# Attention by one head and 128 queries a step, and gates ahead of the branches, in a trunk layer on one Trainium2 core

## The chip, the cores and the metric

The kernel runs on one core of a Trainium2 chip. The metric is the device time of one call in microseconds (us). Each version is run several times on the same chip; a profiled execution beside them gives the trace from which all rows below come. Its times are measured from the start of its span.

## The reference

One layer of a streaming encoder over 1024 positions and 1024 channels, all in float32. A token mixer with three branches is followed by a squared-ReLU MLP; each part is closed by a residual and a layer norm. What matters here is the mixer:

```python
u = layer_norm(x) * (1 + sc_m) + sh_m
z = u @ w_in[l]
z_pool, z_q, z_k, z_v, z_conv, z_gate = jnp.split(z, IN_SPLITS, axis=-1)
y_pool = pool_mixer(z_pool, ...) @ w_br_pool[l]
y_attn = chunk_attention(z_q, z_k, z_v, rel_bias[l]) @ w_br_attn[l]
y_conv = conv_module(z_conv, ...) @ w_br_conv[l]
gates = jax.nn.sigmoid(z_gate + b_gate[l]).reshape(B, S, N_BRANCH, D_MODEL)
merged = gates[:, :, 0] * y_pool + gates[:, :, 1] * y_attn + gates[:, :, 2] * y_conv
mix_out = merged @ w_o[l]
...
# chunk_attention: 8 heads of 64, chunks of 64 queries, keys of the own chunk and 8 before (576)
s = jnp.einsum('bnqhd,bnkhd->bnhqk', q, kb)          # + relative bias, NEG_INF before position 0
p = jax.nn.softmax(s, axis=-1)
o = jnp.einsum('bnhqk,bnkhd->bnqhd', p, vb)
# conv_module: GLU, a depthwise causal convolution of 31 taps on 256 channels, layer norm, swish
```

## The kernel before, in words

Every engine has its own program, written out by hand; semaphores order them against each other. No scheduler is at work: an engine executes its instructions in the order of the code, and waits where the code says `wait_ge`.

TensorE multiplies float32 values as two parts of reduced precision, `x_hi` and `x_lo`. The helper `product` (L1974 to L1976) issues three matmuls for each product: hi by hi, lo by hi, hi by lo. The parts are made in pairs: ScalarE (ACT) copies a raw tile into `_hi`, then VectorE (DVE) subtracts it from the raw tile into `_lo` ("cutting"; weights of `w_in` and of the branches come in blocks of 128 columns, `w_raw`, `w_hi`, `w_lo`, two slots each).

The stages up to the MLP are: the first norm and the projections for pooling and convolution; the projections q, k, v of the first head pair; **attention**; **gates and branches**; the product with `w_o`.

*Attention* is a loop over 64 steps `a` (4 head pairs by 16 chunks). A step takes 64 queries of two heads: their q columns stand block by block in a tile whose other halves are zero (`q_hi`, `q_lo`; GpSimd zeroes them in `zero_q`), so one matmul of 128 rows computes both heads. A step on PE is `scores` (one product, two for the full width of 576 keys in halves of 288), half of `between`, every second step `weigh` (for each block of 128 keys a product of 256 columns), `transpose_probs` of the step before, and the other half of `between`. `between` issues matmuls of 512 columns which project q, k, v for the next pair: 9 a step in the first three pairs, 6 in the last one, where two gate blocks are made ahead (`EARLY`). A gate block is the z_gate projection for 128 channels, 48 matmuls.

On DVE a step adds the bias to the scores and takes the row's maximum (`add_scores`' place, L1523); ACT makes the exponential and the row sum (L997); DVE takes the reciprocal (L1537) and scales the probabilities (L1538); PE transposes them; ACT copies the transposed tile into `pt_hi`, DVE subtracts it into `pt_lo` (L1544). Into nearly every step DVE puts one tap of the convolution (L1428, 62 in all). Six times in a pair DVE cuts half a projection (`take_half_lo`), three times a weight block (`cut_lo`, L1325).

*Gates and branches*: after attention, for each of 8 blocks of 128 channels, PE makes three gate blocks and the three branch products, ACT the sigmoids, DVE the products of both and their sum `mid` (L1602, L1609).

GpSimd (POOL) prepares sums for the MLP: 16 steps in which it loads 256 rows of `w_ff2` (`tw_rows`), multiplies them by the gate row (L778), forms three sums (L783 to L788) and stores them to DRAM (`tw_scratch`). They begin once the first gates, the convolution and the branch inputs are done (L769's waits), so they lie beside gates and branches.

## Time and profile before

| | us |
|---|---|
| device time, median of 3 (lowest, highest) | 1448.37 (1446.94, 1448.57) |
| span of the profiled execution | 1445.0 |
| PE busy | 1426.1 (99%) |
| DVE busy | 966.1 (67%) |
| ACT busy | 586.8 (41%) |
| POOL busy | 455.4 (32%) |

PE's clock was granted in full throughout (a row of 9s), and 96% of the chain that ended last is PE. A busy share of 99% does not say that PE runs at its peak: a matmul's record includes the time in which it overlaps its neighbour. What a matmul occupies is read from the distance between two starts.

In time: attention is 157 to 394 us, gates and branches 394 to about 660 us, POOL's 16 steps 453 to 671 us.

### The profile page before, as it was taken

Reading aid. Unit: us, or ns where it says so; the run is one execution under the profiler, and the core shown is the slowest. Engines: PE = TensorE matmul, PEld = TensorE weight load, DVE = VectorE, ACT = ScalarE, POOL = GpSimd, SP = SyncE. Lnnn points to the kernel's source line nnn. Section 1 sums busy time; section 2 is a strip of 40 time slices with the busy share of each in tenths; the row PEclk is TensorE's granted clock in tenths of the full one; section 3 lists DMA queues with packets and bytes.
Section 4 is the critical chain, followed back from the end, with each engine's and each line's share of the span. In section 5 each row is a group of like instructions: output and inputs, shape, how many; then the busy total and the mean of one; then the engine's idle time right before and its main releaser. Section 6 shows DMA issues by size and latency. Waiting matters only on the chain.

```text
span 1445.0 us, 17546 instructions
## 1 busy us (share of the span) xinstructions
PE 1426.1 (99%) x6770; PEld 1175.9 (81%) x6770; DVE 966.1 (67%) x1242; ACT 586.8 (41%) x829; POOL 455.4 (32%) x381
## 2 busy tenths in 40 slices
PE   7999999999999999999999999999999999999997
PEld 1788888888878888888888898888888888888886
DVE  4888888887785355453468888666555744575594
ACT  3412455555562112112435765444444544443251
POOL 1003500000004889895014415533443302040011
PEclk9999999999999999999999999999999999999999
DMA  9873111101014676776451283544445868576361
GB/s 349 295 265 114 31 30 38 38 16 32 16 44 162 245 259 249 255 268 218 131 204 59 88 277 131 175 154 160 156 137 192 277 243 306 210 233 231 113 224 58
DMA packets 149267, 241.49 MB, mean 167 GB/s; under 512 B 9480, under 2 KB 79550, under 8 KB 147144
## 3 DMA queue, kind: packets, MB, share of 16 engines
q1 hardware_dynamic: 134968, 177.04, 36.7%
q0 software_dynamic: 14224, 63.45, 11.6%
q8 instruction: 47, 0.77, 0.2%
q14 instruction: 28, 0.23, 0.1%
HBM read 170.17 MB, written 70.29 MB: 166 GB/s over the span
## 4 chain that ended last, share of the span: by engine, by line
PE 96%; DVE 1%; DMA 1%; SPq 1%; ACT 0%; issue 0%; DVEq 0%
PE ps L1974 27%; PE ps L1976 27%; PE ps L1975 27%; PE ps L2102 10%; PE ps L2158 2%; DMA mid<-in_x_dram 1%; PE ps L2041 1%; PE ps L2328 0%; SPq L455 0%; DVE bn L1331 0%; PE ps L1993 0%; PE ps L2123 0%; PE ps L2017 0%; PE ps L2200 0%; PE ps L2194 0%; PE ps L2022 0%
## 5 line engine op out<-in xcount | busy, mean ns | idle before, releaser
L1974 PE MATMUL ps<-act_hi,w_hi 128*128 128x512 f32 (+1 forms) x512 | 198.0, 387 | 0.0
L1976 PE MATMUL ps<-act_hi,w_lo 128*128 128x512 f32 (+1 forms) x512 | 196.0, 383 | 0.0
L1975 PE MATMUL ps<-act_lo,w_hi 128*128 128x512 f32 (+1 forms) x512 | 195.9, 383 | 0.0
L1839 DVE TENSOR_TENSOR part_lo<-k_raw,part_hi 128x1024 fp32r<-128x1024 f32 x112 | 153.9, 1414 | 48.2 <-ACT part_hi L872 46.5
L1974 PE MATMUL ps<-part_hi 128*128 128x512 f32 x448 | 174.3, 389 | 0.0
L1975 PE MATMUL ps<-part_lo,part_hi 128*128 128x512 f32 x448 | 174.3, 389 | 0.0
L1976 PE MATMUL ps<-part_hi,part_lo 128*128 128x512 f32 x448 | 174.3, 389 | 0.0
L872 ACT ACTIVATE part_hi<-k_raw 128x1024 fp32r<-128x1024 f32 x112 | 116.3, 1059 | 108.6 <-DMA k_raw<-tw_scratch 84.5
L1571 DVE TENSOR_TENSOR w_lo<-w_raw,w_hi 128x1024 fp32r<-128x1024 f32 x30 | 73.1, 2436 | 123.9 <-ACT w_hi L872 123.8
L1974 PEld LDWEIGHTS ps<-act_hi,w_hi 128*128 128x128 f32 x512 | 96.2, 188 | 19.7 <-issue 1.4
L1975 PEld LDWEIGHTS ps<-act_lo,w_hi 128*128 128x128 f32 x512 | 96.3, 188 | 19.1 <-issue 0.7
L1976 PEld LDWEIGHTS ps<-act_hi,w_lo 128*128 128x128 f32 x512 | 96.2, 188 | 18.9
L1975 PEld LDWEIGHTS ps<-part_lo,part_hi 128*128 128x128 f32 x448 | 84.1, 188 | 17.6
L1974 PEld LDWEIGHTS ps<-part_hi 128*128 128x128 f32 x448 | 84.1, 188 | 17.4
L1976 PEld LDWEIGHTS ps<-part_hi,part_lo 128*128 128x128 f32 x448 | 84.1, 188 | 17.4
L2102 PE MATMUL ps<-act_lo,w_hi 128*128 128x512 f32 x224 | 92.0, 411 | 0.0
L1251 ACT ACTIVATE h_buf<-h_buf,cols 128x1024 f32<-128x1024 f32 x28 | 32.3, 1152 | 144.7 <-DVE h_buf L1834 144.7
L2102 PE MATMUL ps<-act_hi,w_hi 128*128 128x512 f32 x224 | 90.7, 405 | 0.1
L2102 PE MATMUL ps<-act_hi,w_lo 128*128 128x512 f32 x224 | 87.9, 392 | 0.0
L872 ACT ACTIVATE w_hi<-w_raw 128x1024 fp32r<-128x1024 f32 (+1 forms) x53 | 55.6, 1049 | 78.4 <-PE ps L1976 77.3
L1974 PE MATMUL ps<-act_hi,set_hi 128*128 128x512 f32 x224 | 87.1, 389 | 0.0
L1975 PE MATMUL ps<-act_lo,set_hi 128*128 128x512 f32 x224 | 87.1, 389 | 0.0
(261 smaller groups left out, 3243.3 us busy)
## 6 DMA issues: line engine op xcount, KB each, us to landing
k_raw<-h_scratch SPq DMA_DIRECT2D x112, 256.0 KB, 4.0
k_raw<-tw_scratch SPq DMA_DIRECT2D x112, 256.0 KB, 5.0
ada<-in_w_ada_dram SPq DMA_DIRECT2D x11, 2048.0 KB, 8.8
w_raw<-in_w_in_dram SPq DMA_DIRECT2D x42, 512.0 KB, 4.2
tw_rows<-in_w_ff_dram POOLq DMA_DIRECT2D x16, 1024.0 KB, 5.5
tw_scratch<-tw_rows POOLq DMA_DIRECT2D x16, 1024.0 KB, 4.2
h_scratch<-h_sum POOLq DMA_DIRECT2D x64, 256.0 KB, 2.8
pair_raw<-in_w_ff_dram SPq DMA_DIRECT2D x13, 1024.0 KB, 6.0
```

What stands on the lines that cost most here:

```text
L872: return nc.scalar.activation(out, in_, ACT.Copy, **kw)
L1251: nc.scalar.activation(row, row, ACT.Relu, bias=cols[:, R_FF1 + n:R_FF1 + n + 1]).then_inc(relu_done, 1)
L1571: nc.vector.tensor_tensor(w_lo[b % 2][:, :, :], w_raw[b % 2][:, :, :], f(w_hi[b % 2][:, :, :]), ALU.subtract).then_inc(w_lo_done, 1)
L1839: nc.vector.tensor_tensor(part_lo[s][:, :, :], k_raw[rs][:, :, :], f(part_hi[s][:, :, :]), ALU.subtract)\
L1974: nc.tensor.matmul(out, sh, mh, start=first, stop=False)
L1975: nc.tensor.matmul(out, sh, ml, start=False, stop=False)
L1976: return nc.tensor.matmul(out, sl, mh, start=False, stop=last)
L2041: ins = nc.tensor.transpose(ps[:, 2 * (k % 2) + i // 4, (i % 4) * P:(i % 4 + 1) * P], mid[:, i, k * P:(k + 1) * P], ident[:, :])
L2102: ins = nc.tensor.matmul(ps[:, hz % 2, :], s, v, start=kk == 0, stop=kk == 23)
L2158: ins = nc.tensor.transpose(banks(6)[:, b * P:(b + 1) * P], probs[a % 2][:, cs], ident[:, :])
```

## The change

**Attention.** A step is now one head and 128 queries, 64 steps again (pair, head, tile of 128 queries). The scores span 640 keys for 128 queries; the corners outside a query's 576 keys are masked with -1e30 in the bias tile. A tile `qs` holds q's hi part in one head's 64 rows and its lo part in the other 64; `kd` holds the keys twice, in both halves of rows, so one matmul of 128 rows adds q_hi k and q_lo k. The second copy of the keys is made by DMAs within the on-chip memory (`double_keys`, four of 256 KB a pair). Scores are 2 matmuls a part instead of 3. `vs` holds V hi and V lo side by side as the 128 columns of one head, so that `weigh` is one matmul of 256 columns a block of keys; it now stands in every step. The output comes out in pieces: ACT copies one (`take_low`) and DVE adds two (`add_o`). Normalising stays on DVE.

**Projections and gates.** `between` issues 9 matmuls a step in all four pairs (`EARLY` is 3). Behind attention come 18 gate blocks of 48 matmuls (the first within the last two rounds of the attention loop), whose sigmoids are stored to DRAM (512 KB each) and read back; then 8 branch blocks; then the last three gates. The taps are taken out of attention and put between the cuts of the gate blocks.

**GpSimd.** `zero_q` is gone. The `w_ff2` sums are made in 32 steps of half the size, and start when the pooling means are done and the gate rows are stored.

```diff
-EARLY = 2
+EARLY = N_BRANCH
+PIECE = HALF // 2
+TAPS_IN = {0: 5, 1: 2, **{g: 7 for g in range(2, 9)}, 9: 6}
...
             def scores(a):
...
-                    ins = product(ps[:, 4 + part, 0:n],
-                                  ((q_hi[s][:, i, :], q_lo[s][:, i, :]), (k_hi[s][:, ks], k_lo[s][:, ks])),
-                                  True, True)
+                    for term in range(2):
+                        ins = nc.tensor.matmul(ps[:, 4 + part, 0:n], qs[s][:, h, t * P:(t + 1) * P], kd[s][:, term, h, ks],
+                                               start=term == 0, stop=term == 1)
...
-                    ins = product(ps[:, 2, 0:2 * P],
-                                  ((v_hi[s][:, kt, :], v_lo[s][:, kt, :]), (pt_hi[:, pb, :, :], pt_lo[:, pb, :, :])),
-                                  b == 0, b == nb - 1)
+                for m in range(nb):
+                    ins = nc.tensor.matmul(ps[:, 2, (b % 2) * 2 * P:(b % 2 + 1) * 2 * P], vs[s][:, t + 1 - nb + m, h * P:(h + 1) * P],
+                                           pt[:, b % 2, m, :, :], start=m == 0, stop=m == nb - 1)
...
+            def add_o(b):
+
+                pair, h, t = step_of(b)
+                rows = head_rows(h)
+                out = mid[rows, 2 + pair, t * P:(t + 1) * P]
+                dve.wait_ge(o_low_done, b + 1)
+                nc.vector.tensor_tensor(out, o_bank(b, rows, 0), out, ALU.add).then_inc(o_added, 1)
+                dve.wait_ge(o_added, 2 * b + 1)
+                nc.vector.tensor_tensor(out, o_bank(b, rows, 1), out, ALU.add).then_inc(o_added, 1)
...
+            for a in range(N_STEPS + 2):
+                pair, h, t = step_of(a)
                 if a < N_STEPS:
+                    add_scores(a)
+                if half_of(a - 1):
+                    take_half_lo(*half_of(a - 1))
...
+                    nc.vector.reciprocal(inv_sum[:, col:col + 1], row_sum[:, col:col + 1]).then_inc(inv_done, 1)
+                    dve.wait_ge(inv_done, a + 1)
+                    nc.vector.tensor_scalar(probs[a % 2][:, 0:w], probs[a % 2][:, 0:w], inv_sum[:, col:col + 1], None,
+                                            ALU.mult).then_inc(probs_done, 1)
+                if a >= 2:
+                    add_o(a - 2)
+                if 1 <= a <= N_STEPS:
+                    take_pt_lo(a - 1)
...
+            for g in range(G_BLOCKS):
+                cut_lo(N_G + 2 + g)
+                if g == 1:
+                    for k in BR_ORDER[:4]:
+                        cut_branch_lo(k)
+                for n in itertools.islice(taps, TAPS_IN.get(g, 0)):
+                    conv_tap(n)
...
@@ on GpSimd
-            pool.wait_ge(sig_done, EARLY)
-            pool.wait_ge(conv_done, 2)
-            pool.wait_ge(br_lo_done, KT)
-            pool.wait_ge(y_done, 3)
...
+            pool.wait_ge(scratch_stored, 48)
+            pool.wait_ge(means_summed, 8)
+            load_piece(0)
             load_rows(0)
-            for p in range(FF_PAIRS):
+            for u in range(TW_STEPS):
...
@@ on SyncE
+                if m < N_BRANCH:
+                    sp.wait_ge(conv_done, 2)
+                    sp.wait_ge(tw_stored, 32 * TW_STEPS)
```

PE, a full-width step of attention, before (`k_hi`, `q_hi` are the scores' operands, `act`, `w` those of the projections, L2158 the transposes; such steps carry a `weigh` every second time, 15 matmuls `ps<-pt_hi,v_hi`, `pt_lo,v_hi`, `pt_hi,v_lo` of 256 columns):

```order
L1974 MATMUL ps<-k_hi_75,q_hi_71 128x288 [waits biased]
L1975 MATMUL ps<-k_lo_77,q_hi_71 128x288
L1976 MATMUL ps<-k_hi_75,q_lo_73 128x288
L1974 MATMUL ps<-k_hi_75,q_hi_71 128x288
L1975 MATMUL ps<-k_lo_77,q_hi_71 128x288
L1976 MATMUL ps<-k_hi_75,q_lo_73 128x288
L2102 MATMUL ps<-act_hi,w_hi_54 128x512 [waits h_free1]
L2102 MATMUL ps<-act_lo,w_hi_54 128x512
L2102 MATMUL ps<-act_hi,w_lo_56 128x512
L2102 MATMUL ps<-act_hi,w_hi_54 128x512
L2158 MATMUL ps<-ident,probs_86 128x128 [waits pt_lo_done,probs_done]
L2158 MATMUL ps<-ident,probs_86 128x128 x3
```

and PE after, the same place (L2110 scores, L2070 projections, L2135 `weigh`, L2120 transposes):

```order
L2110 MATMUL ps<-kd_73,qs_71 128x320 [waits biased]
L2110 MATMUL ps<-kd_73,qs_71 128x320 x3
L2070 MATMUL ps<-act_hi,w_hi_55 128x512
L2070 MATMUL ps<-act_lo,w_hi_55 128x512
L2070 MATMUL ps<-act_hi,w_lo_57 128x512
L2070 MATMUL ps<-act_hi,w_hi_55 128x512
L2135 MATMUL ps<-pt,vs_75 128x256 [waits o_added,pt_lo_done]
L2135 MATMUL ps<-pt,vs_75 128x256 x2
L2120 MATMUL ps<-ident,probs_80 128x128 [waits pt_lo_done,probs_done]
L2120 MATMUL ps<-ident,probs_80 128x128 x3
L2070 MATMUL ps<-act_lo,w_hi_55 128x512
```

Six score matmuls of 288 columns have become four of 320, and `weigh` stands in each step with 3 to 5 matmuls of 256 columns.

DVE, one full-width step of attention before, beginning with the bias addition:

```order
L1523 ISA probs_85,neg_max<-ps,bias_rev_83 128x576 [waits pt_done,scores_done]
L1523 ISA neg_max 128x1
L1428 SCALAR_TENSOR_TENSOR mid<-h_pad,cols,mid 128x1024 [waits tap_done]
L1537 RECIPROCAL inv_sum<-row_sum 128x1 [waits exp_done]
L1538 TENSOR_SCALAR probs_85<-probs_85,inv_sum 128x576 [waits dve_step]
L1544 TENSOR_TENSOR pt_lo<-ps,pt_hi 128x5x128 [waits pt_hi_done]
```

and after:

```order
L1493 ISA probs_80,neg_max<-ps,bias_rev_78 128x640 [waits pt_done,scores_done]
L1493 ISA neg_max 128x1
L1529 RECIPROCAL inv_sum<-row_sum 128x1 [waits exp_done]
L1531 TENSOR_SCALAR probs_80<-probs_80,inv_sum 128x640 [waits inv_done]
L1503 TENSOR_TENSOR mid<-ps,mid 64x128 [waits o_low_done]
L1505 TENSOR_TENSOR mid<-ps,mid 64x128 [waits o_added]
L1511 TENSOR_TENSOR pt<-ps,pt 128x5x128 [waits pt_hi_done]
```

The tap has gone, the scaling is 64 columns wider, and the two additions from PSUM into `mid` stand ahead of the subtraction that PE's next `weigh` waits for.

DVE in the gate stage after, from the second gate block on (L1309 cuts a weight block, L1412 is a tap):

```order
L1309 TENSOR_TENSOR w_lo_57<-w_raw_53,w_hi_55 128x1024 [waits w_hi_done]
L1408 TENSOR_SCALAR conv_acc<-h_pad,cols 128x1024
L1412 SCALAR_TENSOR_TENSOR conv_acc<-h_pad,cols,conv_acc 128x1024 [waits tap_done] x4
L1309 TENSOR_TENSOR w_lo_56<-w_raw_52,w_hi_54 128x1024 [waits w_hi_done]
L1547 TENSOR_TENSOR br_lo<-mid,br_hi 128x1024 [waits br_hi_done] x4
L1412 SCALAR_TENSOR_TENSOR conv_acc<-h_pad,cols,conv_acc 128x1024 [waits tap_done] x2
L1309 TENSOR_TENSOR w_lo_57<-w_raw_53,w_hi_55 128x1024 [waits w_hi_done]
L1412 SCALAR_TENSOR_TENSOR conv_acc<-h_pad,cols,conv_acc 128x1024 [waits tap_done] x7
L1309 TENSOR_TENSOR w_lo_56<-w_raw_52,w_hi_54 128x1024 [waits w_hi_done]
L1412 SCALAR_TENSOR_TENSOR conv_acc<-h_pad,cols,conv_acc 128x1024 [waits tap_done] x7
```

The taps stand between the cuts of the weights, seven to a gate block from the third on.

POOL before, behind the zeroing of q (`gate_row` is the row of gate values, `tw_rows` the rows of `w_ff2`):

```order
L734 MEMSET q_hi_72 64x16x64 x2
L734 MEMSET q_lo_74 64x16x64 x2
L757 MEMSET w_pool_bd 128x256 [waits scores_done,q_zeroed]
L769 DMA gate_row<-gate_scratch 128x1024 [waits br_lo_done,conv_done,y_done,sig_done,consts_done]
L767 DMA tw_rows_143<-in_w_ff_dram 128x2x1024
L778 TENSOR_TENSOR tw_rows_143<-tw_rows_143,gate_row 128x1024 [waits tw_in]
L778 TENSOR_TENSOR tw_rows_143<-tw_rows_143,gate_row 128x1024
```

and after, behind the pooling means:

```order
L756 TENSOR_TENSOR mid<-mid 64x16 [waits means_summed]
L756 TENSOR_TENSOR mid<-mid 64x16
L777 DMA gate_piece<-gate_scratch 128x256 [waits means_summed,scratch_stored]
L777 DMA gate_piece<-gate_scratch 128x256
L786 DMA tw_rows_143<-in_w_ff_dram 128x2x256 x2
L799 TENSOR_TENSOR tw_rows_143<-tw_rows_143,gate_piece 128x512 [waits tw_in]
L799 TENSOR_TENSOR tw_rows_143<-tw_rows_143,gate_piece 128x512
L786 DMA tw_rows_144<-in_w_ff_dram 128x2x256 [waits tw_summed]
L786 DMA tw_rows_144<-in_w_ff_dram 128x2x256
L807 TENSOR_TENSOR tw_sum_145<-tw_rows_143 128x256
L809 TENSOR_TENSOR tw_sum_145<-tw_rows_143,tw_sum_145 128x256 [waits tw_summed]
```

The first load of `w_ff2` rows no longer waits for the branches; it stands right behind the means, and each operation covers half as many columns.

## Rows read from the trace of the kernel before

**Rows 1.** Busy time by stretch: us, PE, PEld, DVE, ACT, POOL busy, PEclk, DMA share, GB/s.

```profile
0.00:35.00 35.00, 24.60 (x64) 6.13 (x65) 14.04 (x44) 12.50 (x18) 4.11 (x40) 1.00 0.97 348
...
216.00:277.60 61.60, 61.60 (x376) 54.63 (x375) 52.35 (x106) 32.63 (x78) 0.00 (x0) 1.00 0.11 31
```

**Rows 2.** PE's timeline: start us, duration us, engine, line, operation.

```profile
203.83 0.28 PE L1974 MATMUL ps<-pt_hi,v_hi 128*128 128x256 f32 x1
203.95 0.28 PE L1975 MATMUL ps<-pt_lo,v_hi 128*128 128x256 f32 x1
...
207.10 0.40 PE L2102 MATMUL ps<-act_hi,w_lo 128*128 128x512 f32 x1
207.33 0.30 PE L1974 MATMUL ps<-k_hi,q_hi 128*128 128x288 f32 x1
207.46 0.29 PE L1975 MATMUL ps<-k_lo,q_hi 128*128 128x288 f32 x1
```

**Rows 3.** PE's groups by form, whole span: busy us, mean ns, idle before.

```profile
L1976 PE MATMUL ps<-pt_hi,v_lo 128*128 128x256 f32 x120 | 33.9, 282 | 0.0
L1976 PE MATMUL ps<-k_hi,q_lo 128*128 128x288 f32 x64 | 18.9, 295 | 0.0
```

**Rows 4.** PE's timeline, first gate matmul behind attention.

```profile
396.59 0.79 PE L1974 MATMUL ps<-act_hi,w_hi 128*128 128x512 f32 x1
```

**Rows 5.** DVE's timeline, attention steps of 192 and 576 columns, last pair.

```profile
342.59 0.68 DVE L1485 TENSOR_TENSOR v_lo<-ps,v_hi 128x512 fp32r<-128x512 f32 x1
343.19 1.22 DVE L1325 TENSOR_TENSOR w_lo<-w_raw,w_hi 128x1024 fp32r<-128x1024 f32 x1
...
347.02 0.35 DVE L1523 CUSTOM_DVE_ANT_0 probs<-ps,bias_rev 128x192 f32<-128x192 f32 x1
...
348.43 0.28 DVE L1544 TENSOR_TENSOR pt_lo<-ps,pt_hi 128x128 fp32r<-128x128 f32 x1
348.63 0.41 DVE L1523 CUSTOM_DVE_ANT_0 probs<-ps,bias_rev 128x256 f32<-128x256 f32 x1
...
366.35 0.75 DVE L1523 CUSTOM_DVE_ANT_0 probs<-ps,bias_rev 128x576 f32<-128x576 f32 x1
...
368.05 0.17 DVE L1537 RECIPROCAL inv_sum<-row_sum 128x1 f32<-128x1 f32 x1 [0.94 <-ACT probs L997]
368.25 0.52 DVE L1538 TENSOR_SCALAR probs<-probs,inv_sum 128x576 f32<-128x576 f32 x1
368.68 0.82 DVE L1544 TENSOR_TENSOR pt_lo<-ps,pt_hi 128x640 fp32r<-128x640 f32 x1
369.42 0.75 DVE L1523 CUSTOM_DVE_ANT_0 probs<-ps,bias_rev 128x576 f32<-128x576 f32 x1
```

**Rows 6.** Timelines of POOL and DVE where both are busy.

```profile
161.68 1.95 POOL L734 MEMSET q_lo<- 64x1024 f32 x2
162.70 1.02 DVE L1538 TENSOR_SCALAR probs<-probs,inv_sum 128x128 f32<-128x128 f32 x1
...
508.04 4.75 POOL L778 TENSOR_TENSOR tw_rows<-tw_rows,gate_row 128x1024 f32<-128x1024 f32 x2
508.03 5.85 DVE L1609 TENSOR_TENSOR mid<-mid,tmp 128x1024 f32 x1
514.27 1.30 POOL L783 TENSOR_TENSOR tw_sum<-tw_rows 128x512 f32<-128x512 f32 x1
```

**Rows 7.** DVE's groups by form, 455 to 662 us: busy us, mean ns, idle before.

```profile
L1571 DVE TENSOR_TENSOR w_lo<-w_raw,w_hi 128x1024 fp32r<-128x1024 f32 x19 | 59.0, 3105 | 95.2 <-ACT w_hi L872 95.2
L1602 DVE TENSOR_TENSOR tmp<-ps,gate 128x1024 f32<-128x1024 f32 x10 | 12.2, 1225 | 12.3 <-PE ps L1976 11.7
```

**Rows 8.** POOL's timeline, multiplications of its first and its sixteenth step.

```profile
453.58 4.75 POOL L778 TENSOR_TENSOR tw_rows<-tw_rows,gate_row 128x1024 f32<-128x1024 f32 x2 [7.36 <-DMA tw_rows<-in_w_ff_dram]
...
657.23 4.75 POOL L778 TENSOR_TENSOR tw_rows<-tw_rows,gate_row 128x1024 f32<-128x1024 f32 x2
```

**Rows 9.** DVE's timeline, four taps in a row.

```profile
395.23 5.24 DVE L1428 SCALAR_TENSOR_TENSOR mid<-h_pad,cols,mid 128x1024 f32<-128x1024 f32 x4
```

More of the change, by code:

```diff
@@ L491, in _ @@
             load_block(9)
[L492 removed]
+            heads_before = {14: 2, 16: 3, 17: 4, 19: 5, 20: 6, 21: 7}
+            for n in range(10, N_G + 4):
                 if n == 12:
@@ L1111, in cut_row_hi @@
+            for j in range(LAST):
+                cut_hi(N_BR + 2 + j)
             def cut_row_hi(k):
@@ L1529, in _ @@
+            for a in range(N_STEPS + 2):
+                pair, h, t = step_of(a)
+                if a < N_STEPS:
+                    add_scores(a)
+                if half_of(a - 1):
+                    take_half_lo(*half_of(a - 1))
                 if a - MEANS_STEP in range(2):
                     pool_means(1, (a - MEANS_STEP,))
-                elif not late_cut(a) and a not in NO_TAP:
-                    for n in range(2 if a == N_STEPS else 1):
-                        conv_tap(tap)
-                        tap += 1
+                elif a == STEPS * (PAIRS - 1):
+                    nc.vector.memset(w_pool_bd[:, :, :], 0.0).then_inc(consts_done, 2)
```

1039 lines of the change are left out of this document (474 added, 565 removed).

## The prediction, as it stood before the changed kernel ran

> **What bounds the kernel now.** I read the shares of the page, then busy time by stretch, then PE's starts, and last DVE and POOL where they meet. By stretch, a pair of attention takes 61.60 us and PE is busy in all of it, while DVE is busy 52.35 [rows 1]. PE's starts stand at fixed distances: 0.23 us after a matmul of 512 columns, 0.13 after one of 288, 0.12 after one of 256 [rows 2]. So PE is full in attention, and DVE follows within nine microseconds a pair. A matmul saved is a gain only as far as DVE is not what PE waits for next. From here each stage has two candidates, PE and DVE, and I price both.
>
> **PE in attention.** The scores of a full-width step are six matmuls of 288 columns before, four of 320 after. Before there are 8 such steps a pair, 32 in all, 192 matmuls; the row of one of the three terms shows its 64 [rows 3]. 192 x 0.133 = 25.5 us. The narrow ones (widths 64 to 512, 24 a pair) I put between 0.10 and 0.23 by interpolation from [rows 2], 14.1 in all; together 39.6. After there are 128 of 320 columns; from 0.133 at 288 and 0.23 at 512 the interpolation gives 0.147, so 18.8, and 32 narrow ones (128 to 512) 10.2; together 29.0. Saved: 10.6. Weighing is 3 x 120 matmuls of 256 columns [rows 3], 43.2 us at 0.12; after it is one for each of five blocks or fewer in each of 64 steps, 240, 28.8. Saved: 14.4. Transposes stay 240 and projections stay the same number. PE's work falls by 25.0 us. The gate matmuls between steps (9 in all pairs) only change place. A pair after is 61.60 - 6.2 = 55.4 us of PE. In the transition to the gates one gate matmul lasts 0.79 where its like lasts 0.40, a wait of 0.4 [rows 4, 2]; I count 4 us for several such waits between 350 and 450 us (bounds 1 and 5), which go since the taps no longer end there.
>
> **DVE in attention.** Its chain in a step is closed: bias and maximum, a wait of 0.94 for ACT's exponential, reciprocal, scaling, then the subtraction, and then the next step; without a tap or a cut the loop is 369.42 - 366.35 = 3.07 us [rows 5]. PE's step before is 61.6 / 16 = 3.85, so a tap of 1.31 [rows 9] fitted in part into the wait for ACT. After, the score tile is 640 instead of 576. For the price of a column I take two loops: 3.07 at 576 and 348.63 - 347.02 = 1.61 at 192. Of these 0.74 and 0.20 are the subtraction over 640 and 128 columns, so the rest grows by 0.92 in 384 columns, 0.0024 each, and the subtraction by 0.00105 each. The extra 64 columns are 0.15. The two additions of the output (128 columns from PSUM) are like the 128-column subtraction, 0.20 each [rows 5], and the second waits for the first: 0.25 each. The full step is 3.07 + 0.15 + 0.50 = 3.72; the narrow ones average 320 columns, 3.72 - 320 x 0.00345 = 2.62. A pair: 8 x 3.72 + 8 x 2.62 = 50.7, two V subtractions of 0.60 [rows 5] 1.2, three weight cuts of 1.13 (1.22 in [rows 5], less the overlap with its neighbour) 3.4, and the halves of q and k, two instructions of 512 columns each (1.2) of which 0.94 lies in the wait for ACT, 0.3 by four, 1.2. Sum 56.5 against PE's 55.4. So even undisturbed DVE is now the longer one, by 1.1 us a pair. The taps are what leaves; had they stayed, the loop would be far longer.
>
> **The port.** What comes in beside it is POOL. Before, attention has no POOL work after its first steps (0.00 in the stretch shown, [rows 1]). Where both are busy, DVE pays: an addition with both inputs in SBUF lasts 5.85 beside POOL's pair of multiplications of 4.75, starting and ending with it; and the scaling of 128 columns lasts 1.02 beside a POOL memset, where 576 columns take 0.52 alone [rows 5, 6]. In 455 to 662 us the weight cut averages 3.105 instead of 1.22, so each waits 1.88, while the product that reads PSUM stays at 1.225 [rows 7]. So I charge waits to the scaling (16 a pair) and the cuts (3), and none to instructions that read PSUM.
> The Trainium skill, page "SBUF — State Buffer", section "Who interferes with whom", says that VectorE and GpSimd share one port pair as an exclusive lock for a whole instruction, and that an instruction of VectorE with at most one SBUF input outside the two-port modes doesn't contend. The trace agrees for the products from PSUM (1.225). The scaling, with one SBUF input, would by that page be safe outside those modes and blocked in them; the 1.02 beside the memset says the latter. By the safe reading only the 12 cuts would wait, 1.1 + 1.5 a pair or 10 us in all, and the sum would be 1453.
> The size: a POOL step before is (657.23 - 453.58) / 15 = 13.6 us [rows 8]. After, its operations are halved: the pair of multiplications 2.4, sums 0.65 each instead of 1.30 [rows 6], with their starts 0.1 more, in runs of 2.6, 0.75, 1.5, 0.75. DMA issues and semaphores do not halve, so I put the step between 9.9 and 12, at 10.6. An instruction that arrives anywhere waits (2.6^2 + 0.75^2 + 1.5^2 + 0.75^2) / (2 x 10.6) = 0.48. Scaling the measured 1.88 by a quarter for the runs' squares and by 13.6 / 10.6 for the cycle gives 0.60. I take 0.5 and keep 0 (all fall between POOL's runs) and 0.65. A pair: 19 x 0.5 = 9.5 on top of 56.5 is 66.0, less PE's 55.4: 10.6 us in which PE waits, 43 in four pairs. Lower bound 4 x 1.1, say 5 to 8 with uneven steps; upper 19 x 0.65 = 12.4, 54 in four pairs.
> POOL starts when the pooling means are ready, about where attention starts, and needs 32 x 10.6 = 339 us. Attention ends near 157 + 4 x 66 = 421 us, so about 25 steps are through and 7 to 8 run beside the first gates.
>
> **The gate stage.** A gate block is 48 matmuls, 11.2 us of PE at 0.2325. DVE has to fit seven taps of 1.31 [rows 9] and a cut of 1.13 into it: 10.3. That fits alone. But taps and cuts have two SBUF inputs, all eight. When both engines want the port all the time, a POOL step takes its 9.9 plus some 1.07 for each of four runs that wait for a DVE instruction, 14.2, of which POOL holds the port 5.6 and DVE has 8.6, or 0.61: a block takes 10.3 / 0.61 = 17 us. Eight steps of 14.2 are 114 us, 6.7 blocks; the first two have fewer taps (5 and 2, but four branch cuts), so some 5.7 blocks fall behind by 5.8 each: 33. The cuts run one block ahead, which hides 11.2 less a tap and a bit, 9.5. PE waits 24 us. Bounds: with a POOL step of 9.9 only 5 are left, 10; with 12, 10 are left, 39; with no conflict 0. The rest of the stage I cost at nothing: means and variance of the convolution are at the 12th and 14th block, the sums at the ninth end; sigmoids go out in 11 us intervals with the queue free; reading them back waits for POOL's last store, near 421 + 114 = 535 us, while 18 blocks last until past 620. If that cover goes, every microsecond of delay counts in full. The key copies wait a step or two before each pair; the halves they need are made early enough, except the last, which I hold inside the lower end.
>
> **Sum.** 1445.0 (this execution's span) - 25.0 - 4 + 43 + 24 = 1483; the median lies 3.4 above the span: 1486.
>
> **Rivals.**
> B, the attention waits alone: POOL is faster than I think or DVE makes up its lateness with the lighter ninth block, so that the gate stage is hidden. 1445.0 - 25 - 4 + 43 + 3.4 = 1462. For it: the block alone has 0.9 us of room. Against it: eight instructions of two inputs a block.
> C, faster: DVE's instructions fall between POOL's. DVE's loop is tied to PE's step of about 3.5 us and POOL is held up instead; the price is then only the lower bound of 8: 1445.0 - 25 - 4 + 8 + 3.4 = 1427. Of the 29 us saved, 4 go in DVE's own length, so it decides where the gate stage is hidden and the mean wait of the 76 port instructions in attention is below 25 / 76 = 0.33 us. For it: most of POOL's runs are 1.5 or less. Against: 1.88 each in [rows 7].
> D, another stall: the sigmoids' way through DRAM, the key copies, or the clock. PE would now wait in most steps, 0.7 us in 4.1, and a lower clock would double what follows. Against the clock: in the first 35 us PE is busy 24.60 and the granted clock is 1.00, 2.4 GHz [rows 1].
> The Trainium skill, page "TensorE: Matmul & The Clock Gate", section "Part 1: The HAM clock gate (the "warmup" mystery)", has an idle TensorE fall back to half its clock; by that rule stretches of attention could run at 1.2 GHz, and the row just named did not show it.
> With one pair's PE work at the lower clock it is 55 us more; a small part of that, or a late read, gives 1475 to 1515, which I put at 1500.
>
> **Chances.** The forecast has 0.57, B 0.20, C 0.15, D 0.08. A measurement of this kernel tells 0.2% (2.9 us) from no change; only the upper edge of C and the lower edge of B land there, 0.01 of the one and 0.02 of the other. Faster 0.14, within 0.2% 0.03, slower 0.57 + 0.18 + 0.08 = 0.83. The forecast's own range is 1472 (1445 - 25 - 4 + 43 + 10 + 3.4) to 1512 (54 and 39 come together seldom; I end at 1508). With B, and short of C, the range is 1440 to 1508; outside are C's 0.15 and 0.03 above.
>
> **What would show it.** Right: PE's stretches of a pair near 66 us with PE's matmuls starting late after DVE's subtraction; the scaling at 0.5 plus some 0.5 on average; POOL steps of 10 to 12 us from about 157 us; in the gate stage cuts and taps lasting twice their time until POOL ends near 535, then 11.2 us a block. Wrong: pairs near 56 us, or the scaling at 0.55 throughout (C); gate blocks of 11.2 from the start (B); a granted clock under 1.00 or idle time behind a DMA in the branch blocks (D).

## The result, and the profile after

The changed kernel takes 1522.79 us (median of 4, 1517.33 to 1526.81), the kernel before on the same chip 1447.86 us. The ratio is 1.0515, 95% interval [1.049, 1.054]: slower by 75 us. I had forecast 1486, and at most 1508. The sign was right, the size was half.

The page of the changed kernel: the span, each engine's busy time, and PE with its clock in 40 slices.

```profile
span 1525.0 us, 17398 instructions
PE 1433.0 (94%) x6554; PEld 1167.3 (77%) x6554; DVE 1050.1 (69%) x1378; ACT 598.4 (39%) x838; POOL 537.0 (35%) x553
...
PE   6998978777879999999999999999999999999998
...
PEclk9999989999999999999999999999999999999999
```

PE has 216 matmuls fewer and 80 us more span. Its holes lie in slices 6 to 12, which is attention. The chain that ended last shows who fills them; before, PE had 96% of it:

```profile
PE 66%; DVE 23%; issue 4%; ACT 3%; DMA 3%; SPq 1%; POOL 1%; DVEq 0%; ACTq 0%; POOLq 0%
```

What PE waits for in attention (engine, tile, whom it waits for: us in total, times, longest):

```profile
PE ps L2135 <- DVE pt L1511: 55.8, 32, 3.6
PE ps L2110 <- DVE neg_max L1493: 4.6, 3, 2.1
```

So PE stands at `weigh` and waits for the subtraction of the transposed tile, in 32 of the 64 steps. The busy time of the two stages (columns as in [rows 1]), first of before, then of after:

```profile
156.80:393.60 236.80, 236.55 (x1444) 208.56 (x1443) 197.66 (x407) 126.48 (x302) 6.62 (x10) 1.00 0.10 28
393.60:726.90 333.30, 333.30 (x1465) 273.30 (x1464) 175.37 (x110) 88.30 (x92) 200.24 (x145) 1.00 0.58 200
```

```profile
164.70:484.70 320.00, 258.91 (x1329) 213.63 (x1328) 253.51 (x494) 139.52 (x313) 244.20 (x282) 0.94 0.52 163
484.70:806.40 321.70, 314.99 (x1363) 257.22 (x1362) 213.84 (x165) 85.51 (x88) 44.24 (x40) 0.99 0.44 148
```

Attention has grown from 237 to 320 us, POOL has come in with 244 us, and the granted clock is 0.94. The busy shares still hide part of PE's waits, so I took every distance between two starts of PE and compared it with the usual one for the form in front (its median). What is longer is a wait, or, where the granted clock is at its lower level and the distance is doubled, work at half speed. In us, from one profile of each kernel, with the median time of its runs (the kernel before was at 1447.9 to 1448.4 beside all of them):

| kernel | attention starts | attention: work, waits, half-clock loss | gates and branches: work, waits, half-clock loss | median |
|---|---|---|---|---|
| before | 156.8 | 232.9, 3.9, 0.0 | 330.3, 3.1, 0.0 | 1447.9 |
| after | 164.7 | 228.9, 79.5, 11.7 | 308.7, 10.4, 2.5 | 1522.8 |
| e1_narrow | 163.4 | 228.9, 24.2, 0.0 | 308.7, 6.2, 0.0 | 1454.9 |
| e2_act | 162.0 | 228.9, 44.3, 1.2 | 308.7, 20.5, 3.2 | 1493.0 |
| e3_means | 159.3 | 228.9, 81.4, 15.5 | 308.7, 6.4, 1.5 | 1522.5 |
| e4_read | 164.7 | 228.9, 85.3, 16.3 | 308.7, 2.9, 0.0 | 1519.0 |
| e5_order | 164.6 | 228.9, 25.2, 0.0 | 308.7, 24.4, 10.7 | 1483.8 |
| e6_load | 164.1 | 228.9, 26.2, 0.0 | 308.7, 29.2, 8.8 | 1485.9 |
| e7_limit | 159.5 | 228.9, 19.0, 0.0 | 308.7, 2.9, 0.0 | 1439.7 |
| e8_all | 158.0 | 228.9, 30.0, 1.3 | 308.7, 21.6, 7.3 | 1476.8 |
| e9_taps | 158.3 | 228.9, 37.5, 5.7 | 308.7, 9.0, 2.4 | 1464.6 |
| e10_noadd | 162.7 | 228.9, 11.6, 0.0 | 308.7, 7.3, 1.2 | 1442.1 |
| e11_split | 162.9 | 228.9, 48.9, 1.0 | 308.7, 18.1, 1.5 | 1497.3 |
| e12_final | 159.2 | 228.9, 25.8, 0.0 | 308.7, 16.2, 0.0 | 1460.6 |

Two cautions. e4 has the changed kernel's code up to the end of attention and lost 101.6 us there against 91.2, so one profile tells the loss of a kernel like this to about 10 us. And the split between waits and half-clock loss depends on where a doubled distance is drawn; it moves by 3 to 4 us, and in e12 some of the 16.2 was work at the lower level (0.50 at 559 to 562). The sum of the two does not move.

The 80 us between the two spans are: work -25.6, waits in attention +75.6, half-clock loss there +11.7, gates and branches +7.3 and +2.5, the time ahead of attention +7.9, the rest +0.6.

Where the waits come from is seen in one step. DVE after, the step that answers to the one in [rows 5], undisturbed:

```profile
301.41 0.81 DVE L1493 CUSTOM_DVE_ANT_0 probs<-ps,bias_rev 128x640 f32<-128x640 f32 x1
...
303.22 0.17 DVE L1529 RECIPROCAL inv_sum<-row_sum 128x1 f32<-128x1 f32 x1 [0.99 <-ACT probs L1024]
303.42 0.55 DVE L1531 TENSOR_SCALAR probs<-probs,inv_sum 128x640 f32<-128x640 f32 x1
304.01 0.29 DVE L1503 TENSOR_TENSOR mid<-ps,mid 64x128 f32<-64x128 f32 x1
304.34 0.29 DVE L1505 TENSOR_TENSOR mid<-ps,mid 64x128 f32<-64x128 f32 x1
304.66 0.82 DVE L1511 TENSOR_TENSOR pt<-ps,pt 128x640 fp32r<-128x640 f32 x1
305.40 0.81 DVE L1493 CUSTOM_DVE_ANT_0 probs<-ps,bias_rev 128x640 f32<-128x640 f32 x1
```

This step is one of a pair's second head; its loop is 3.99 us, not 3.72. And one beside POOL, DVE, then POOL, then PE:

```profile
339.23 3.44 DVE L1531 TENSOR_SCALAR probs<-probs,inv_sum 128x640 f32<-128x640 f32 x1
342.59 0.27 DVE L1503 TENSOR_TENSOR mid<-ps,mid 64x128 f32<-64x128 f32 x1
```

```profile
338.23 0.78 POOL L813 DMA_DIRECT2D tw_scratch<-tw_rows  x1
339.00 0.77 POOL L815 DMA_DIRECT2D tw_scratch<-tw_sum  x1
339.79 2.52 POOL L799 TENSOR_TENSOR tw_rows<-tw_rows,gate_piece 128x512 f32<-128x512 f32 x2
```

```profile
340.91 0.40 PE L2070 MATMUL ps<-act_hi,w_hi 128*128 128x512 f32 x1
343.96 0.86 PE L2135 MATMUL ps<-pt,vs 128*128 128x256 f32 x5 [2.65 <-DVE pt L1511]
```

The scaling begins at 339.23, while POOL issues a store, and ends 0.3 us after POOL's second multiplication; PE waits 2.65 us for what stands behind it on DVE.

### The profile page after: what moved, and what is told of

It reads as the page before. It is cut to its first block, busy times and chain, and to the rows that moved or that the text cites. A ratio compares the mean times of both kernels' runs of the same rounds, so it can differ in the third digit from the quotient of the medians.

```text
span 1525.0 us, 17398 instructions
## 1 busy us (share of the span) xinstructions
PE 1433.0 (94%) x6554; PEld 1167.3 (77%) x6554; DVE 1050.1 (69%) x1378; ACT 598.4 (39%) x838; POOL 537.0 (35%) x553
## 4 chain that ended last, share of the span: by engine, by line
PE 66%; DVE 23%; issue 4%; ACT 3%; DMA 3%; SPq 1%; POOL 1%; DVEq 0%; ACTq 0%; POOLq 0%
PE ps L1942 20%; PE ps L1944 20%; PE ps L1943 20%; DVE probs L1531 5%; PE ps L2070 2%; DVE w_lo L1309 2%; DVE pt L1511 2%; DVE probs L1493 2%; DVE conv_acc L1412 2%; DVE bn L1315 1%; DVE partial L1354 1%; DMA mid<-in_x_dram 1%; DVE mid L1683 1%; ACT probs L1024 1%; DVE mid L1503 1%
## 5 line engine op out<-in xcount | busy, mean ns | idle before, releaser
L1942 PE MATMUL ps<-act_hi,w_hi 128*128 128x512 f32 (+1 forms) x496 | 192.7, 389 | 3.4 <-DVE w_lo L1309 3.2
L1944 PE MATMUL ps<-act_hi,w_lo 128*128 128x512 f32 (+1 forms) x496 | 190.2, 384 | 0.0
L1943 PE MATMUL ps<-act_lo,w_hi 128*128 128x512 f32 (+1 forms) x496 | 190.1, 383 | 0.0
L1309 DVE TENSOR_TENSOR w_lo<-w_raw,w_hi 128x1024 fp32r<-128x1024 f32 x52 | 75.8, 1459 | 66.3 <-ACT w_hi L888 66.3
L1024 ACT ACTIVATE probs<-probs,neg_max 128x640 f32<-128x640 f32 (+2 forms) x64 | 44.6, 696 | 158.5 <-DVE neg_max L1493 158.5
L2070 PE MATMUL ps<-act_lo,w_hi 128*128 128x512 f32 x240 | 104.8, 437 | 0.0
L2070 PE MATMUL ps<-act_hi,w_hi 128*128 128x512 f32 x240 | 98.9, 412 | 4.0 <-DVE kd L1457 2.9
L2135 PE MATMUL ps<-pt,vs 128*128 128x256 f32 x240 | 46.1, 314 | 56.5 <-DVE pt L1511 55.8
L2070 PE MATMUL ps<-act_hi,w_lo 128*128 128x512 f32 x240 | 98.1, 409 | 0.0
L2135 PEld LDWEIGHTS ps<-pt,vs 128*128 128x128 f32 x240 | 36.2, 202 | 76.2 <-DVE pt L1511 74.4
```

The source lines that it names most:

```text
L1024: nc.scalar.activation(probs[a % 2][:, 0:w], probs[a % 2][:, 0:w], ACT.Exp, bias=neg_max[:, col:col + 1], scale=-1.0, accum_out=row_sum[:, ...
L1309: nc.vector.tensor_tensor(w_lo[n % 2][:, :, :], w_raw[n % 2][:, :, :], f(w_hi[n % 2][:, :, :]), ALU.subtract).then_inc(w_lo_done, 1)
L1942: nc.tensor.matmul(out, sh, mh, start=first, stop=False)
L1943: nc.tensor.matmul(out, sh, ml, start=False, stop=False)
L1944: return nc.tensor.matmul(out, sl, mh, start=False, stop=last)
L2070: ins = nc.tensor.matmul(ps[:, hz % 2, :], s, v, start=kk == 0, stop=kk == 23)
```

## The experiments

All but e1, e7 and e10 compute the full result.

**e1_narrow: is it POOL's operations?**

```diff
-nc.gpsimd.tensor_tensor(pair, pair, gate_piece[:, :, :], ALU.mult)
+nc.gpsimd.tensor_tensor(pair[:, :, 0:8], pair[:, :, 0:8], gate_piece[:, :, 0:8], ALU.mult)
-nc.gpsimd.tensor_tensor(sums[:, 0, :], b12, b11, ALU.subtract)       # and the three others
+nc.gpsimd.tensor_tensor(sums[:, 0, 0:8], b12[:, 0:8], b11[:, 0:8], ALU.subtract)
-nc.gpsimd.dma_start(tw_dram[p, :, 4:7, cs], sums[:, :, :])
+nc.gpsimd.dma_start(tw_dram[p, :, 4:7, cs], rows[:, 0:3, :])
```

> GpSimd's six operations of a w_ff2 step cover 8 columns instead of 256 or 512 (so the sums for the MLP are not computed); its DMAs stay as they are. Theory P (DVE's scaling and weight cuts wait for GpSimd's runs, and those waits are most of PE's idle time): the scaling and the cuts wait 0.84 us on average in attention, 64 us in all; with runs of only DMA issues left the wait falls to 0.1 to 0.3, PE's waits in attention fall from 80 to 25 to 35 us, the clock stays up, and the time is 1455 to 1470. Rival L (DVE's own loop of 3.99 us and its place ahead of the weighing is what PE waits for): scaling gets shorter but PE's waits stay above 60 and the time above 1500. Rival D (the DMA issues hold the port as long as the operations do): the scaling still waits over 0.5 on average, time about 1490.

1454.91 us, ratio 1.0055 [1.0038, 1.0072]. Theory P holds. Two groups of DVE in attention (busy, mean ns), first of the changed kernel, then of e1:

```profile
L1531 DVE TENSOR_SCALAR probs<-probs,inv_sum 128x640 f32<-128x640 f32 x32 | 44.9, 1402 | 1.1
L1309 DVE TENSOR_TENSOR w_lo<-w_raw,w_hi 128x1024 fp32r<-128x1024 f32 x13 | 24.0, 1850 | 0.0
```

```profile
L1309 DVE TENSOR_TENSOR w_lo<-w_raw,w_hi 128x1024 fp32r<-128x1024 f32 x19 | 23.1, 1217 | 12.4 <-ACT w_hi L888 12.4
L1531 DVE TENSOR_SCALAR probs<-probs,inv_sum 128x640 f32<-128x640 f32 x32 | 18.2, 568 | 1.1
```

The scaling falls from 1.40 to 0.57, the cut from 1.85 to 1.22. Measured against e1's duration at the same width, the 64 scalings lose 52.6 us in the changed kernel, 0.82 each. With POOL's operations short, 55 of the 79.5 us of waits in attention go, and all of the half clock. Rival D falls: DMA issues alone cost the scaling nothing (eleven began while a store was being issued and waited 0.06 on average). What also shows is that the rest is no gain either: 24.2 us of waits remain against the 25.6 us of work saved, and attention starts 6.6 us late.

**e2_act, e5_order: the scaling leaves DVE.**

```diff
 # ScalarE, behind exp(a) and take_low(a - 2)
+                if a < N_STEPS:
+                    act.wait_ge(inv_done, a + 1)
+                    copy(probs[a % 2][:, 0:w], probs[a % 2][:, 0:w], scale=inv_sum[:, col:col + 1]).then_inc(probs_done, 1)
                 if 1 <= a <= N_STEPS:
                     take_pt_hi(a - 1)        # in e5_order this stands ahead of the scaling
 # VectorE
-                    nc.vector.tensor_scalar(probs[a % 2][:, 0:w], probs[a % 2][:, 0:w], inv_sum[:, col:col + 1], None,
-                                            ALU.mult).then_inc(probs_done, 1)
```

> The probabilities are scaled by ScalarE instead of VectorE; everything else as in the changed kernel, GpSimd's stage included. Theory P: the 64 scalings take their waits (53 us) and their own 0.55 with them; DVE's loop falls to about 3.4 us, below PE's 3.83, only the 12 cuts still wait; PE's waits in attention fall from 80 to 10 to 20 us and the half-clock stretches go: 1435 to 1450. Rival L2 (the chain of a step, scores to transposes, is what counts, and ACT adds 0.7 plus two hand-overs to it): PE still waits 30 us or more, 1460 to 1480. Rival N (the gate stage or the start takes the place): attention is short but the rest grows, above 1460.

1492.97 us, ratio 1.0319 [1.0302, 1.0336]. Better by 30 us, but 50 short of theory P: rivals L2 and N both have a part. The subtraction now waits for ACT, whose copy is queued behind the scaling:

```profile
255.69 0.71 ACT L888 ACTIVATE pt<-ps 128x640 fp32r<-128x640 f32 x1
...
260.31 0.83 ACT L888 ACTIVATE probs<-probs,inv_sum 128x640 f32<-128x640 f32 x1
261.17 0.70 ACT L888 ACTIVATE pt<-ps 128x640 fp32r<-128x640 f32 x1
```

```profile
261.90 0.82 DVE L1514 TENSOR_TENSOR pt<-ps,pt 128x640 fp32r<-128x640 f32 x1 [0.89 <-ACT pt L888]
```

> As the run with the scaling on ScalarE, but ScalarE copies the transposed tile of the step before (pt_hi) ahead of the scaling instead of behind it. Theory K (in that run PE waited 28 us for the subtraction pt, which waited 0.9 to 1.0 us a step for a copy queued behind the scaling): the waits in attention fall from 44 us to 10 to 18; attention ends some 30 us earlier, GpSimd's steps do not, so that the gate stage waits more, 25 to 28 instead of 20: 1465 to 1475. Rival A (ScalarE is full, or the hand-over DVE to ACT is the cost): attention waits stay above 35, time 1485 to 1495.

1483.78 us, ratio 1.0266 [1.0229, 1.0303]. The direction of theory K is right, its size is not: attention's waits fall from 44.3 to 25.2, where 10 to 18 were expected; no half clock is left, and attention is 20 us shorter. The gate stage takes half of it back, and there the half-clock loss was not expected: waits 20.5 to 24.4, half-clock loss 3.2 to 10.7. The time misses the expected range by 9 us. A POOL step does not get shorter with POOL's operations (11.6 us in the changed kernel, 11.5 in e1), so a shorter attention leaves more steps beside the taps: nine begin behind attention in e5, seven in e2. In e5 PE waits there for the weight cuts, which stand behind taps:

```profile
PE ps L1942 <- DVE w_lo L1312: 14.8, 6, 4.0
PE ps L1942 <- DVE mid L1608: 3.8, 1, 3.8
```

**e3_means: why attention starts late.**

```diff
             pool.wait_ge(zp_done, 2)
+            pool.wait_ge(partial_done, 12 - N_DIRECT)
             pool.wait_ge(pooled_done, 2)
```

> GpSimd's second pooling means wait again for the last of VectorE's conditioning products, as they did before the change (the wait had gone with the zeroing of q). Theory S: attention starts 8 us late since these means ran at 124 to 139 us beside VectorE's weight cut (2.91 instead of 1.22) and its conditioning products (7.46 instead of 5.48), PE then waited 4 us and fell to half its clock for some microseconds; with the wait it starts at 157 to 160 us and the time falls by 4 to 7 us, to about 1517. Rival: the start is late for the order in which VectorE now makes the halves of q and k, and nothing changes (1522 plus or minus 3). GpSimd's w_ff2 steps begin later by a few us, which costs at most 2.

Attention starts at 159.3 instead of 164.7, and at 158 to 159.5 in the four others that have this edit (e7, e8, e9, e12): the start of theory S is confirmed. The total is not: 1522.53 us, ratio 1.0506 [1.0487, 1.0524], where about 1517 was expected. In this profile attention lost 5.7 us more; that is inside the 10 us between profiles of the same code, so the total shows neither a gain nor a loss.

**e4_read: the sigmoids' way back.**

```diff
                 load_block(N_G + 4 + g)
-            for m in range(2 * N_BRANCH):
+                if g == VAR_BLOCK:
+                    for m in range(N_BRANCH):
+                        load_sigmoid(m)
+            for m in range(N_BRANCH, 2 * N_BRANCH):
                 load_sigmoid(m)
```

> The first three stored sigmoids are read back after the 15th gate block instead of behind the last store on SyncE's queue. Theory R: PE's wait of 3.7 us at 691 us and the half clock behind it (2.5 us of loss) come from this queue order; time falls by 5 to 6 us, to 1517. Rival: the second read of three (which waits for a later store) is what comes late next, and only 0 to 2 us are gained.

The wait of the changed kernel is a transfer that comes in late behind SyncE's queue:

```profile
693.31 1.23 DVE L1608 TENSOR_TENSOR mid<-ps,gate_back 128x1024 f32<-128x1024 f32 x1 [9.66 <-DMA gate_back<-sig_scratch]
...
694.68 0.76 PE L1942 MATMUL ps<-br_hi,w_hi 128*128 128x512 f32 x1 [3.52 <-DVE mid L1608]
```

With the edit the stage's waits are 2.9 and nothing is lost to the clock, as theory R says. The total, 1519.00 us, ratio 1.0480 [1.0460, 1.0500], is 3.8 us less by median, but its interval overlaps the changed kernel's; the stage is shown, the total is not.

**e6_load: can POOL be made faster?**

```diff
-                if u >= 1:                                  # behind the multiplications
-                    pool.wait_ge(tw_stored, 32 * u)
-                if u + 1 < TW_STEPS:
-                    load_rows(u + 1)
                 nc.gpsimd.tensor_tensor(sums[:, 1, :], ...)
+                ...                                         # the same four lines here
```

> The same with GpSimd's wait for the store before last and its next loads moved from behind the multiplications to behind the second sum. Theory G: GpSimd's step of 11.5 us is set by its DMAs (it was 11.5 with the operations narrowed to 8 columns too), of which 1.3 to 3 us are the wait for the store; with the wait moved the step is 9.8 to 10.5, the stage ends 35 to 50 us earlier, and the gate stage waits 8 to 12 us less than in the run beside it. Rival: the loads then land late and the step stays at 11.5 or grows; no change.

1485.94 us, ratio 1.0265 [1.0248, 1.0282]. Theory G falls. A POOL step is 11.95 us, in e5 beside it 11.91. POOL's idle time ahead of its loads falls from 1.9 to 0.2 us a step, and ahead of the store's issue it grows from 0.4 to 1.9; what POOL waits for there the profile does not name.

**e7_limit and e8_all: the parts together, without and with POOL's work.**

> Scaling on ScalarE with the copy first, GpSimd's operations on 8 columns (the MLP's sums are not computed), its later start of the means, and the first sigmoids read earlier: what the new order of work takes when the port is free. Theory: PE's work is 25 us less and nothing waits much: 1425 to 1432. Rival: DVE's additions and cuts still hold PE, 1438 to 1445.

> All that computes the full result: scaling on ScalarE with the copy first, GpSimd's loads moved, the means' later start, the first sigmoids read earlier. From the parts: the time of the run with the loads moved less 5 (start of attention) less 4 (read): 1450 to 1460, which would be near the kernel before but not faster. Rival: if the gate stage no longer waits, 1438 to 1445, faster than before.

e7 1439.67 us, ratio 0.9942 [0.9925, 0.9958]: the rival's range; 19 us of waits in attention stay. So even without POOL's operations beside it, and with the scaling on ACT, the new order gives 8 us, not 25. e8 1476.80 us, ratio 1.0196 [1.0177, 1.0214], above what I expected, since the load part did nothing and the gate stage still loses 28.9 us.

**e9_taps: thinner taps beside POOL** (scaling and order of e5, edits of e3 and e4).

```diff
-MEAN_BLOCK, VAR_BLOCK = 12, 14
-TAPS_IN = {0: 5, 1: 2, **{g: 7 for g in range(2, 9)}, 9: 6}
+MEAN_BLOCK, VAR_BLOCK = 14, 16
+TAPS_IN = {0: 4, 1: 1, **{g: 5 for g in range(2, 10)}, 10: 7, 11: 7, 12: 3}
```

> Scaling on ScalarE with the copy first, the means' later start, the first sigmoids read earlier (GpSimd's loads where they were), and the taps spread thinner: 4, 1, then five to a gate block up to the 9th and seven after it, with the convolution's mean at block 14 and its variance at 16 instead of 12 and 14. Theory W: beside GpSimd a block of seven taps and a cut takes DVE about 17 us against PE's 11.2, one of five taps 12.6; so the 24 us of waits and the 11 us of half-clock loss of the gate stage fall to under 8 in all, and the time is 1445 to 1455. Rival V: GpSimd's stage is held up less by DVE but no wait disappears since every cut itself waits for a GpSimd run, 1465 to 1475. Rival U: the late end of the convolution delays the branch blocks, more waits at 680 us.

1464.62 us, ratio 1.0103 [1.0082, 1.0124]. The waits for the cuts in the gate stage are gone, as theory W says; 11.4 us are lost there instead of under 8, of which 5.5 is one wait for a branch cut (`br_lo`) behind the late convolution (rival U). The nearest kernel for comparison is e8, which also has the edits of e3 and e4 but the thick taps: it lost 28.9. The total missed theory W's range by 10 us. The profile is of the slowest of the four runs (1470.9) and lost 43 us in attention, where e5 lost 25 and e8 31 with nearly the same order of work; why is not shown.

**e10_noadd: the price of an addition** (on e1).

```diff
-                nc.vector.tensor_tensor(out, o_bank(b, rows, 0), out, ALU.add).then_inc(o_added, 1)
-                dve.wait_ge(o_added, 2 * b + 1)
-                nc.vector.tensor_tensor(out, o_bank(b, rows, 1), out, ALU.add).then_inc(o_added, 1)
+                nc.vector.tensor_tensor(out, o_bank(b, rows, 0), out, ALU.add).then_inc(o_added, 2)
```

> As the run with GpSimd's operations on 8 columns (scaling on DVE), with the second of the two output additions left out (the product with V's low part is missing from the output, and the MLP's sums). It prices my undersized term: DVE's full loop is 3.99 us instead of the 3.72 forecast, mainly since each addition takes 0.33 instead of 0.25 and the scaling 0.59. Without one addition the loop is 3.66, below PE's 3.83: PE's waits in attention fall from 24 us to 10 to 15, the time by 9 to 14, to about 1444. Rival: PE waits at the steps with a cut or a half alone, which one addition doesn't cure; waits fall by under 6.

1442.13 us, ratio 0.9964 [0.9950, 0.9978], 12.8 us less than e1; the waits in attention fall from 24.2 to 11.6. So one addition is half of the remainder that POOL did not explain. Whose the other half is, no run separates: full steps without a cut now take 3.33 to 3.84 on DVE, but each pair still has one of 4.7 to 5.1 with a cut in it.

**e11_split: where DVE gets in** (on the changed kernel).

```diff
                 for i in range(2):
                     pair = rows[:, 2 * i:2 * i + 2, :]
+                    if i == 1 and u >= 1:
+                        ...
+                        nc.gpsimd.dma_start(tw_dram[...], tw_sum[(u - 1) % 2][:, :, :]).then_inc(tw_stored, 16)
                     nc.gpsimd.tensor_tensor(pair, pair, gate_piece[:, :, :], ALU.mult).then_inc(tw_summed, 1)
...
-                nc.gpsimd.dma_start(tw_dram[p, :, 4:7, cs], sums[:, :, :]).then_inc(tw_stored, 16)   # stays in the last step
```

> The changed kernel with GpSimd's second store of a step issued between the two multiplications of the next step instead of ahead of them. In the changed kernel 14 of 64 scalings began while these stores were being issued and ended only with the second multiplication, 2.5 to 3.3 us later, and make up 37 us of the 53. Theory H (DVE gets the port when GpSimd does something else than an operation between two, however short): runs of 2.5 become 1.3, the mean wait of the scaling falls from 0.84 to about 0.5, attention waits fall from 80 to 55 to 65: 1495 to 1508. Rival J (the issue of a DMA holds the port in effect as well when an operation stands behind it): the wait stays, time 1520 to 1530, or longer by GpSimd's longer step.

1497.32 us, ratio 1.0354 [1.0331, 1.0376]: 25 us less than the changed kernel by moving one DMA issue. The scalings' lost time falls from 52.6 to 24.0 us, with POOL's step in attention unchanged at 11.4. Rival J falls for the moved issue: six scalings began while it lasted, with POOL's second multiplication behind it, and waited 0 to 0.5 us. (Two began in the issue that still stands ahead of the first multiplication, and waited 2.1 and 2.2.) One of the six, POOL and then DVE:

```profile
414.74 1.31 POOL L804 TENSOR_TENSOR tw_rows<-tw_rows,gate_piece 128x512 f32<-128x512 f32 x1
415.97 0.80 POOL L802 DMA_DIRECT2D tw_scratch<-tw_sum  x1
416.79 1.56 POOL L804 TENSOR_TENSOR tw_rows<-tw_rows,gate_piece 128x512 f32<-128x512 f32 x1
```

```profile
416.33 0.91 DVE L1537 TENSOR_SCALAR probs<-probs,inv_sum 128x640 f32<-128x640 f32 x1
```

The scaling waited 0.36 us and the second multiplication lasted 1.56 instead of 1.3. A scaling that comes in the first multiplication waits for that one alone:

```profile
313.02 1.30 POOL L804 TENSOR_TENSOR tw_rows<-tw_rows,gate_piece 128x512 f32<-128x512 f32 x1
314.26 0.80 POOL L802 DMA_DIRECT2D tw_scratch<-tw_sum  x1
```

```profile
313.11 2.17 DVE L1537 TENSOR_SCALAR probs<-probs,inv_sum 128x512 f32<-128x512 f32 x1
```

It began at 313.11 and ended at 315.28; alone this width takes 0.49, so its work fell into the issue, ahead of the second multiplication (315.08 to 316.4). Theory H's time holds (1495 to 1508 was expected); the mean wait, 0.37, and the waits in attention, 48.9, came out below its 0.5 and 55 to 65.

**e12_final: all that helped**, with `TAPS_IN` 4, 2, five up to block 8, then seven, and mean and variance at 13 and 15.

> All of the parts that helped: scaling on ScalarE with the copy first, the means' later start, the first sigmoids read earlier, taps thinner beside GpSimd (4, 2, five a block to the 8th, then seven; mean at block 13, variance at 15), and GpSimd's second store between its two multiplications. Theory: the run with the taps spread (1464.6) less 5 us for the late convolution it waited for at its end and 5 to 12 us for shorter waits of cuts and halves: 1448 to 1457, no better than the kernel before. Rival: waits of cuts and taps fall as those of the scaling did (by half): 1438 to 1446, faster than the kernel before.

1460.56 us (median of 5), ratio 1.0097 [1.0083, 1.0112]. It is the fastest full version of the new kind and slower than the kernel before, and 4 us above the range expected. Attention waits 25.8; the gate stage has one wait that my tap schedule made, since the convolution's sums came late:

```profile
PE ps L2167 <- DVE conv_sig L1577: 10.9, 1, 10.9
```

Without it the sum would be near 1450, by subtraction. That was not run.

## Why the prediction was wrong, point by point

The forecast was 38 us slower, the measurement 75 (80 between the two profiled spans). Two terms of attention were too small: DVE's own loop (4.4 us of waits forecast, 24.2 left in e1) and the wait at the port (38 forecast; 55.3 is what e1 takes away). Two terms stood at nothing: the clock (11.7) and the time ahead of attention (7.9). One was too large, the gate stage (24 forecast, 9.8 lost), and by luck it hid 14 us of the others.

**PE's work, -25.0: right.** Measured -25.6 over both stages. (The 32 narrow score matmuls of the forecast are 64; their 10.2 us was the price of 64.) The kernel before had 7.0 us of waits in the two stages, most of them of 0.1 or 0.2 us; whether the 4 us that the forecast takes off went can't be told from the new waits.

**DVE's own loop: too small.** The prediction put the full step at 3.72. Where POOL is quiet, the first head of a pair takes just that, as in e1 (the end of the step that begins at 180.32):

```profile
182.32 0.55 DVE L1531 TENSOR_SCALAR probs<-probs,inv_sum 128x640 f32<-128x640 f32 x1
182.79 0.28 DVE L1503 TENSOR_TENSOR mid<-ps,mid 64x128 f32<-64x128 f32 x1
183.10 0.28 DVE L1505 TENSOR_TENSOR mid<-ps,mid 64x128 f32<-64x128 f32 x1
183.31 0.81 DVE L1511 TENSOR_TENSOR pt<-ps,pt 128x640 fp32r<-128x640 f32 x1
184.04 0.81 DVE L1493 CUSTOM_DVE_ANT_0 probs<-ps,bias_rev 128x640 f32<-128x640 f32 x1
```

The second head, whose output lies in rows 64 to 127 of `mid`, takes 3.99: there nothing overlaps the additions, which stand 0.33 and 0.32 from the next start instead of 0.31 and 0.21, and the scaling ahead of them 0.59 instead of 0.47. Why the rows matter no run tests. The other miss is the halves of q and k: I had left 0.3 of each outside the wait for ACT; in e1 they put the reciprocal off by 0.46 in a full step (2.27 behind the bias addition instead of 1.81) and by 0.77 in a step of 128 columns (1.62 instead of 0.85). A pair in e1 takes 61.0 us from 238.31 to 299.30, where I had summed 56.5 for DVE and 55.4 for PE. Of e1's 24.2 us of waits, e10 shows that one addition is worth 12.6.

**The mean wait at the port: with what it did to the clock, the step that failed most.** I had 0.5 us for each of 76 instructions, from runs of 2.6, 0.75, 1.5, 0.75 in a POOL step of 10.6. The step was near (11.4 us in attention); the wait was 0.82 for the scaling (52.6 / 64) and 0.65 for the cut (8.4 / 13). Fourteen scalings began while a store was being issued; 13 of them waited 2.5 to 3.3 us, which is 37 of the 52.6 us. For them the run was not 2.6 but 4.1: two issues, 1.5 us, and both multiplications. With 4.1 for 2.6 and 11.4 for 10.6 the forecast's own formula gives 0.89, an estimate from these rows. My bound of 0.65 came from scaling the measured mean by a quarter; a run that has issues in it doesn't shrink so. (The row behind that mean was read too simply: the addition beside POOL lasted 5.85 because it waited out POOL's 4.75 and then took its own time, so it ended 1.1 us after POOL's row and not with it.)
What is shown: POOL's operations cause the waits (e1), and parting the run halves the loss (e11). What stays open is why an issue ahead of the multiplications holds DVE (13 of 14 cases here, both cases in e11), while an issue with 8-column operations behind it (e1) or one between the two multiplications (e11) does not. Spans on POOL are rough, so an operation may begin earlier than its row says.

**The gate stage, +24: the mechanism is there, the amount was not.** In the changed kernel it was 7.3 of waits and 2.5 of half clock more than before, 3.7 of the waits from the sigmoids' read, which I had held for hidden. Attention was so slow that only four POOL steps and the rest of a fifth lay beside the gates, not eight. Where attention was shorter, such an amount appeared: 24.4 and 10.7 us in e5, with nine steps left; and with thin taps it went (28.9 in e8, 11.4 in e9). That the waits in e5 equal my 24 is chance, since its attention is another one. The two stages share one debt: what POOL has not done in attention is paid at the gates.

**The clock, rival D: held for improbable, and there.** Behind a long wait the granted clock falls to half, 1.2 GHz (columns as in [rows 1]):

```profile
213.00:216.00 3.00, 0.54 (x4) 0.12 (x2) 2.84 (x7) 0.96 (x1) 1.64 (x4) 0.97 0.12 26
...
216.00:219.00 3.00, 3.00 (x10) 2.61 (x11) 2.85 (x8) 1.58 (x4) 2.84 (x4) 0.50 0.48 165
```

In attention 37.5 us ran at the lower level; 11.7 us were lost by it. It did not follow each long wait: of 16 waits of 2 us and more in attention nine had a fall behind them and seven had none, such as the wait of 2.65 shown above (1.00 at 344 to 347). e1's attention, with no wait above 1.4 us, has 1.00. The row of the first 35 us [rows 1], which I set against it, was one profile's: in e1's the same stretch has 0.95. The Trainium skill, page "TensorE: Matmul & The Clock Gate", section "Part 1: The HAM clock gate (the "warmup" mystery)", says that an idle TensorE falls to half its clock; here the trace agrees, and I should have given the rule more than a small part of 0.08.

**Ahead of attention: priced at nothing, 7.9 us.** With the zeroing of q went two waits that had held POOL's second pooling means back. They ran at 124 to 139 us instead of from 143, beside DVE's cut (2.91 instead of 1.22) and its conditioning products (7.46 instead of 5.48). e3 puts the wait back and has 5.4 us of it; the other 2.5 stay open.

**The rivals.** B asked for a hidden gate stage and C also for a mean wait below 0.33; neither came. e7, with POOL's operations cut to 8 columns and the scaling on ACT, is the nearest to C and gave 1439.7, not 1427: 19 us of waits in attention remained, at least 8.1 of them for DVE's subtraction.

## What to carry to other kernels

When PE's work is cut and a vector engine's chain is within a few per cent of PE's (here 56.5 against 55.4 us a pair by my sum), that chain has to be priced from start to start, for each kind of step, since all of PE's gain (25.6 us) can go back in it (24.2 in e1). Before moving a background stage of another engine beside a critical one, ask which instructions of the critical engine use the port both share, and how long the longest uninterrupted run of the background engine is, its DMA issues included: by the sum above the mean wait goes with the square of the run, and a DMA issue moved from ahead of two operations to between them was worth 25 us. A wait that is deleted with the work it protected may have been holding something else back in time.
